# Row halves of the PE array in turn for RWKV preparation, and four quadrants for the token-pair products of the scan

## The chip, the cores and the metric

The kernel runs on one NeuronCore of a Trainium2 chip. The metric is device time in microseconds (us) of one execution. The kernel before was timed three times: 3051.62, 3055.73 and 3055.89 us, median 3055.73 us. Its profiled execution took 3055.24 us, of which the span of the trace is 3053.4 us; the remaining 1.8 us lie around the span.

## The reference

One inference step of a two-layer decoder. Each layer has three token mixers in parallel (retention, differential attention, RWKV-7), which are merged by gates, and an MLP. 512 prompt tokens and 8 single-token sequences (T = 520 columns) share all weights. The change touches only the RWKV-7 mixer. Cut to what matters (L is the layer, 8 heads of 64 channels):

```python
zs = z_rwkv + (zprev - z_rwkv) * mu_shift
rc, kc, vc, wd, ad, gd = split(zs)                      # 512, 512, 512, 64, 64, 160 columns
w = -softplus(-(w0 + tanh(wd) @ w_decay_up)) - 0.5      # contraction over 64
decay = exp(-exp(w))
vgate = sigmoid(v0 + (vc @ w_v_down) @ w_v_up)          # 512 -> 32 -> 512
vc = vc + (v_first - vc) * vgate                        # second layer only
a = sigmoid(a0 + ad @ w_a_up)                           # contraction over 64
kk = normalised(kc * k_k);  kc = kc * (1 + (a - 1) * k_a)
for t in tokens:                                        # S is 64 x 64 per head
    S = S * decay_t + (S @ -kk_t) outer (kk_t * a_t) + v_t outer k_t
    y_t = S @ r_t
y = groupnorm(y) + sum(r * k * r_k) * v                 # sum(r*k*r_k) is the "bonus"
```

The prompt scan is computed in chunks of 64 tokens. Within a chunk it needs the products of every pair of tokens, for every head: (b, a), (b, r), (k, a), (k, r), each a 64x64 block, then the inverse of a triangular matrix, then the update of the state chunk by chunk.

## The kernel before, in words

The layer body is one loop iteration; it consists of blocks, and all five engines meet at the end of each. Channels lie on partitions and tokens on columns for all of the preparation; a 520-column row is handled as two halves of 260 (`TH`), half h in PSUM banks 4h to 4h+3. All matmuls here are float32, and each appears in the trace as two MATMUL records, each with its LDWEIGHTS record, all at line 381 (transposes at 384). A form such as `64*128 64x260` means 64 rows and 128 columns of weights, and a moving operand of 260 columns. Engines order themselves by semaphores; `dv(...)` and `ac(...)` make VectorE and ScalarE wait for their own last instruction.

**The preparation block** (from line 1652) runs in this order. PE turns the previous rows, then adds up the squares of k for each head into four 32-column groups of the output (`pair32`). After that `up_tile` (line 1709) makes nine tiles: for n = 1 to 4 tanh(wd) times `w_decay_up` on rows 0 to 63, for n = 5 to 8 ad times `w_a_up` on rows 64 to 127. They alternate between two banks (`pair(n)`), and ScalarE's `tile` (line 1761) reads each with a sigmoid (`L1768`) and frees the bank. When all eight are read, ScalarE forms a factor (`L1794`), VectorE multiplies k by it (`L1876`), scans the decays (`L1880`) and scales kk by its norm (`L1886`). PE then makes `vc @ w_v_down`, eight matmuls of 32 output columns that add up in rows 0 to 31 of one bank pair. ScalarE copies these 32 rows (`L1770`), and four `up_tile` calls with 32 rows of weights give the gate of v, each read by a sigmoid. VectorE blends v (`L1896`, `L1898`) and forms r*k*r_k (`L1900`). PE sums that over heads with 20 small matmuls into bank 5 (the bonus), then turns 40 blocks of `dvec`, the operands of the 8 single tokens. VectorE forms z2 (`L1909`), waits for the bonus, copies it (`L1912`, `L1913`), multiplies z1, k and r by decays (`L1915`, `L1916`, `L1919`), and splits the turned blocks (`L1923`). SyncE issues the loads of the block's weights in the order of the code, and PE waits for all of them with one count (`loaded`, six loads of 16).

**A block for the eight single tokens** follows, which the change leaves alone.

**The scan block** (from line 2049) handles four groups m of 128 tokens, two chunks cc of 64 each. `products(left, right, m, bank, g)` makes for one row half g (channels of the even or the odd heads) eight 64x64 blocks: the rows of the array are those of g, the columns are those of cc, and cc alternates. The two calls of a pair (g = 0, then g = 1) write to two neighbouring banks. For each m: the blocks of (b, a) and (b, r) come first, then (k, a), five levels of `head_products` with masks on VectorE between them, (k, r) inside level 1, then for each cc the right-hand side, the update, the output and the new state. The (b, a) or (b, r) products of m+1 stand inside that last part: g = 0 ahead of the wait for `rhs_copied` and g = 1 behind the matmuls for `u`. VectorE masks (`L2164`, `L2185`), adds (`L2199`, `L2201`), copies the right-hand side (`L2206`) and `u` (`L2208`) and updates the state (`L2215`).

Of the kernel before, what the change touches and what calls it, by code (L numbers as in the profile page):

```python
# [20 lines left out]
ACT = mybir.ActivationFunctionType  # L21
AX = mybir.AxisListType

P = 128
# [3 lines left out]
MT = SEQ // P  # L28
DEC = 8
T = SEQ + DEC  # L30
TH = T // 2
# [6 lines left out]
HC, DC = 8, 64  # L38
HP = HC // 2
# [165 lines left out]
def build(nc, a, consts, outs):  # L205
# [6 lines left out]
    V, S, G, PE = nc.vector, nc.scalar, nc.gpsimd, nc.tensor  # L212
    with ExitStack() as ctx:
# [166 lines left out]
        def mm(out, lhsT, rhs, start=True, stop=True):  # L380
            return PE.matmul(out, lhsT, rhs, start=start, stop=stop, skip_group_check=True)  # L381
# [133 lines left out]
        with nc.Fori(0, DEPTH) as l:  # L515
# [1050 lines left out]
            w_g1, w_g2 = ring[1][:, 512:1024], ring[1][0:32, 1024:1536]  # L1566
            w_vu = ring[1][0:32, 1536:2048]
            w_vd = at(ring[1], 2048, HP, 32)
# [81 lines left out]
            ds_ = at(ring[0], 0, DEC, HP, DC)  # L1650
            decay_rate = -math.exp(-0.5)
            with nc.Block() as block:
                @block.sync
                def _(sp):
                    sp.dma_start(w_up2[0:64, :], L("w_decay_up")).then_inc(loaded, 16)
                    sp.dma_start(w_up2[64:128, :], L("w_a_up")).then_inc(loaded, 16)
                    sp.dma_start(w_vu, a["w_v_up"][0]).then_inc(loaded, 16)
                    sp.dma_start(w_vd, a["w_v_down"][0].rearrange("(k p) n -> p k n", p=P)).then_inc(loaded, 16)
                    sp.wait_ge(prev_turned, 1)
                    sp.dma_start(y3.rearrange("p k t -> p (k t)"), v_spill).then_inc(v_first_loaded, 16)  # L1660
                    wg = L("w_g_up")
# [12 lines left out]
                    sr = L("state_rwkv").rearrange("b (q g) i j -> g i b q j", g=2)  # L1674
                    for g in range(2):
                        for b in range(DEC):
                            sp.dma_start(ds_[g * 64:(g + 1) * 64, b], sr[g, :, b]).then_inc(states_loaded, 16)
                    sp.wait_ge(loaded, c["loaded"].base + 96)
                    sp.wait_ge(stored, c["stored"].next(32))
# [4 lines left out]
                def _(pe):  # L1684
# [13 lines left out]
                    def pair(n):  # L1698
                        return (pb[n % 2][:, 0:TH], pb[4 + n % 2][:, 0:TH])
# [8 lines left out]

                    def up_tile(n, lhs, rows_, rhs, ct):
                        for half in range(2):  # L1710
                            t = mm(pair(n)[half], lhs[rows_, ct * P:(ct + 1) * P], rhs[rows_, half * TH:(half + 1) * TH])
                        t.then_inc(up_made, 1)

                    pe.wait_ge(loaded, c["loaded"].base + 96)
                    pe.wait_ge(rows_copied, 3)
                    for n in range(1, 9):
                        if n >= 2:
                            pe.wait_ge(up_read, n - 1)
                        up_tile(n, w_up2, slice(0, 64) if n < 5 else slice(64, 128), wdad, (n - 1) % 4)

# [12 lines left out]
                    for half in range(2):  # L1733
                        for k in range(HP):
                            t = mm(pair(1)[half][0:32], w_vd[:, k, :], v_[:, k, half * TH:(half + 1) * TH],
                                   start=(k == 0), stop=(k == HP - 1))
                    t.then_inc(up_made, 1)
                    pe.wait_ge(kk_scaled, 4)
                    for ct in range(HP):
                        pe.wait_ge(up_read, 10 + max(0, ct - 1))  # L1740
                        up_tile(ct, w_vu, slice(0, 32), vdn, ct)

                    pe.wait_ge(dve_for_pe, c["pe_from_dve"].next())
                    for m in range(5):
                        r = P if m < MT else DEC
                        for hp in range(HP):
                            t = mm(pb[5][0:r, m * 8 + hp * 2:m * 8 + hp * 2 + 2], y3[:, hp, m * P:m * P + r], C("pair"))
                    t.then_inc(pe_for_dve, 1)
                    pe.wait_ge(dve_for_pe, c["pe_from_dve"].next())
                    for n in range(5):  # L1750
                        for hp in range(HP):
                            for g in range(2):
                                gs, c0 = slice(g * 64, (g + 1) * 64), n % 2 * 256 + hp * DC
                                t = mm(pb[n // 2][32 * g:32 * (g + 1), c0:c0 + DC], dvec[gs, n, hp, :], ident[gs, gs])
                    t.then_inc(pe_for_act, 1)

                @block.scalar
                def _(s):
# [26 lines left out]
                    for n in range(1, 9):  # L1785
                        ct = (n - 1) % 4
                        tile(n, n % 2, (z0 if n < 5 else z1)[:, ct], ACT.Sigmoid, name=PR("w0" if n < 5 else "a0")[:, ct:ct + 1])
                        if n in (4, 8):
                            S.sem_inc(act_for_dve, 1)


# [5 lines left out]
                    
                    tile(9, 1, vdn, ACT.Copy, rows_=32)
                    s.wait_ge(dve_for_act, c["act_from_dve"].next())
# [23 lines left out]
                def _(v):  # L1823
# [86 lines left out]
                    V.sem_inc(dve_for_act, 1)  # L1910
                    v.wait_ge(pe_for_dve, c["dve_from_pe"].next())
                    V.tensor_copy(bonus[:, 0:MT], at(pb[5], 0, MT, HC))  # L1912
                    dv(V.tensor_copy(bonus[0:DEC, MT], pb[5][0:DEC, MT * 8:MT * 8 + 8]))  # L1913
                    v.wait_ge(act_for_dve, c["dve_from_act"].next())
# [5 lines left out]
                    for i in range(3):  # L1920
# [3 lines left out]
                                           tokv[0][:, nn].bitcast(F32), sub))  # L1924
            c["loaded"].skip(96)

# [122 lines left out]
            with nc.Block() as block:  # L2049

                @block.tensor
                def _(pe):
                    def products(left, right, m, bank, g):

                        gs = slice(g * 64, (g + 1) * 64)
                        for hp in range(HP):
                            for cc in range(2):
                                tok = slice(m * P + cc * CH, m * P + (cc + 1) * CH)
                                t = mm(at(pb[bank + g], 0, HP, CH)[lower[cc], hp], left[gs, hp, tok], right[gs, hp, tok])
                        return t  # L2060
# [7 lines left out]

                    products(z1, z2, 0, 4, 0)
                    products(z1, z2, 0, 4, 1).then_inc(ba_made, 1)  # L2070
                    products(z1, r_, 0, 6, 0)
                    products(z1, r_, 0, 6, 1).then_inc(br_made, 1)
                    for m in range(MT):
# [8 lines left out]
                        pe.wait_ge(ba_masked, m + 1)  # L2082
                        products(k_, z2, m, 4, 0)
                        products(k_, z2, m, 4, 1).then_inc(ka_made, 1)
                        for lv in range(1, 6):
# [6 lines left out]
                            if lv == 1:  # L2092

                                pe.wait_ge(br_masked, m + 1)
                                products(k_, r_, m, 6, 0)
                                products(k_, r_, m, 6, 1).then_inc(kr_made, 1)
                            for g in range(2):
# [10 lines left out]
                        for cc in range(2):  # L2108
# [15 lines left out]
                            if m + 1 < MT:  # L2124
                                products(z1, (z2, r_)[cc], m + 1, 4 + 2 * cc, 0)
                            pe.wait_ge(rhs_copied, n + 1)
                            for h, hp, g, hs, gs in heads:
                                t = mm(pb[1][r, hs], xt[r, g, hp], rhs1[r, hs])
                            t.then_inc(u_made, 1)
                            if m + 1 < MT:  # L2130
                                products(z1, (z2, r_)[cc], m + 1, 4 + 2 * cc, 1).then_inc((ba_made, br_made)[cc], 1)
                            if n:
# [587 lines left out]
```

## Time and profile before

| | |
|---|---|
| median of 3 runs | 3055.73 us (3051.62 to 3055.89) |
| profiled execution | 3055.24 us, span 3053.4 us, mean granted clock of TensorE 0.895 |
| PE busy | 2675.8 us, 88% of the span |
| VectorE busy | 1466.5 us, 48% |
| ScalarE busy | 828.7 us, 27% |
| preparation block, first layer | about 708 to 786.5 us |
| single-token block, first layer | about 786.5 to 831.6 us |
| scan block, first layer | from 831.6 us to about 987 us |

Times in a trace are counted from the start of the span. The granted clock is a share of full speed: 1.00 is 2.4 GHz and 0.50 is 1.2 GHz. In a timeline, `xN` merges N neighbouring instructions, whose duration is from the start of the first to the end of the last, and the bracket gives the idle time of the engine just before and what ended it. Matmuls are pipelined, so the busy share of PE does not tell how full its array is.

### The profile page before, as it was taken

The numbers are of one execution on the slowest core, as the hardware profiler recorded it, in microseconds if no ns is written. First come the engines' busy times: TensorE is split into PE (matmuls) and PEld (weight loads), VectorE is DVE, ScalarE is ACT, GpSimd is POOL, SyncE is SP. The second block draws the span as 40 slices with busy tenths as digits, with TensorE's granted clock in tenths as the row PEclk, the third lists the DMA queues.
The fourth block names the chain that finished last, engine by engine and source line by source line (L and its number), as shares of the span: only waits on it lengthen the run. The fifth ranks groups of instructions, "written<-read, shape, count | busy, mean of one in ns | idle before, by whom it ended". The sixth has DMA issues, their size and how long they took to land. (4 is left out here: it accounts for less than half of the span.)

```text
span 3053.4 us, 52943 instructions
## 1 busy us (share of the span) xinstructions
PE 2675.8 (88%) x22778; PEld 2336.9 (77%) x22778; DVE 1466.5 (48%) x2077; ACT 828.7 (27%) x1232; POOL 164.0 (5%) x102
## 2 busy tenths in 40 slices
PE   5988888997698898999979879798958979799998
PEld 3777665895587698999956767577936859799998
DVE  4253256434755765334351632734366566633343
ACT  1311224223310332333232112332241114232331
POOL 0021010300000000000000210112000000000000
PEclk8987899996599799999989879889956979899999
DMA  7222245711000442222341331655010015322223
GB/s 290 69 66 78 88 166 191 224 45 53 15 3 4 144 161 76 91 84 84 138 150 35 87 117 46 232 183 178 21 48 15 3 45 181 111 84 83 84 83 139
DMA packets 216308, 305.14 MB, mean 100 GB/s; under 512 B 28021, under 2 KB 97191, under 8 KB 214786
## 3 DMA queue, kind: packets, MB, share of 16 engines
q1 hardware_dynamic: 216066, 301.67, 29.6%
q8 instruction: 182, 2.98, 0.4%
q14 instruction: 60, 0.49, 0.0%
HBM read 266.49 MB, written 35.14 MB: 99 GB/s over the span
## 5 line engine op out<-in xcount | busy, mean ns | idle before, releaser
L381 PE MATMUL pb<-h_high,f_high 128*128 128x260 f32 x1984 | 400.9, 283 | 4.9 <-DVEq L2641 4.9
L381 PE MATMUL pb<-h_low,f_high 128*128 128x260 f32 x1984 | 398.1, 282 | 0.0
L381 PE MATMUL pb<-h_high,f_low 128*128 128x260 f32 x1920 | 387.2, 283 | 0.0
L556 DVE TENSOR_TENSOR w_low<-ring,w_high 128x2048 fp32r<-128x2048 f32 x66 | 151.3, 2292 | 379.2 <-ACT w_high L548 377.8
L381 PEld LDWEIGHTS pb<-h_high,f_high 128*128 128x128 f32 x1984 | 305.7, 188 | 5.3 <-issue 5.3
L381 PEld LDWEIGHTS pb<-h_low,f_high 128*128 128x128 f32 x1984 | 307.1, 189 | 0.0
L556 DVE TENSOR_TENSOR f_low<-ring,f_high 128x2048 fp32r<-128x2048 f32 x60 | 137.6, 2293 | 337.1 <-ACT h_high L550 212.8
L381 PEld LDWEIGHTS pb<-h_high,f_low 128*128 128x128 f32 x1920 | 294.0, 188 | 0.0
L763 POOL TENSOR_TENSOR g_low<-yT,g_high 128x512 fp32r<-128x512 f32 x96 | 161.8, 1691 | 1942.6 <-ACT g_high L759 1942.6
L548 ACT ACTIVATE f_high<-ring 128x2048 fp32r<-128x2048 f32 x62 | 118.8, 1916 | 350.9 <-PE pb L381 326.5
L381 PE MATMUL pb<-arena 64*64 64x64 f32 (+4 forms) x2320 | 190.8, 302 | 23.7 <-DVE arena L987 9.4
L548 ACT ACTIVATE w_high<-ring 128x2048 fp32r<-128x2048 f32 x66 | 126.1, 1916 | 308.1 <-PE pb L381 185.7
L381 PE MATMUL pb<-h_high,g_high 128*128 128x260 f32 x768 | 165.9, 299 | 41.6 <-POOL g_low L763 21.9
L381 PE MATMUL pb<-w_high,h_high 128*128 128x512 f32 x448 | 183.2, 409 | 21.7 <-DVEq L560 11.6
L381 PE MATMUL pb<-h_high,w_high 128*128 128x260 f32 x800 | 167.4, 292 | 31.6 <-DVE h_low L2535 17.1
L381 PEld LDWEIGHTS pb<-arena 64*64 64x64 f32 (+4 forms) x2320 | 143.6, 170 | 59.3 <-issue 39.2
L381 PE MATMUL pb<-w_high,h_low 128*128 128x512 f32 x448 | 179.9, 401 | 0.0
L381 PE MATMUL pb<-w_low,h_high 128*128 128x512 f32 x448 | 179.8, 401 | 0.0
L381 PEld LDWEIGHTS pb<-h_high,g_high 128*128 128x128 f32 x768 | 124.1, 198 | 60.8 <-POOL g_low L763 38.9
L381 PE MATMUL pb<-h_high,w_low 128*128 128x260 f32 x800 | 165.1, 288 | 0.0
L381 PE MATMUL pb<-h_low,w_high 128*128 128x260 f32 x800 | 164.9, 288 | 0.0
L381 PE MATMUL pb<-h_low,g_high 128*128 128x260 f32 x768 | 160.0, 291 | 0.0
(368 smaller groups left out, 4631.6 us busy)
## 6 DMA issues: line engine op xcount, KB each, us to landing
ring<-in_w_ff_dram SPq DMA_DIRECT2D x32, 2048.0 KB, 8.0
ring<-in_w_in_dram SPq DMA_DIRECT2D x20, 2048.0 KB, 8.9
ring<-in_w_ada_dram SPq DMA_DIRECT2D x18, 2048.0 KB, 8.4
yT<-in_w_in_dram SPq DMA_DIRECT2D x96, 256.0 KB, 3.5
arena<-in_w_ada_dram SPq DMA_DIRECT2D x9, 2048.0 KB
gate_spill_dram<-yT SPq DMA_DIRECT2D x48, 260.0 KB, 4.1
arena<-gate_spill_dram SPq DMA_DIRECT2D x12, 1040.0 KB, 5.3
arena<-in_cache_k_diff_dram SPq DMA_DIRECT2D x32, 256.0 KB, 3.0
```

The lines of the kernel that those rows point to most:

```text
L381: return PE.matmul(out, lhsT, rhs, start=start, stop=stop, skip_group_check=True)
L548: t = S.activation(ws[n % 2][0], ring[slot][:, u * 2048:(u + 1) * 2048], ACT.Copy)
L556: t = V.tensor_tensor(ws[n % 2][1], ring[slot][:, u * 2048:(u + 1) * 2048], ws[n % 2][0].bitcast(F32), sub)
L763: G.tensor_tensor(g_split[j % 2][1], g_raw[j % 2], g_split[j % 2][0].bitcast(F32), sub).then_inc(gate_ready, 1)
```

## The change

In the preparation, the tiles of decay (rows 0 to 63) and of a (rows 64 to 127) are made in pairs over four bank pairs. The down-projection of v no longer adds up its four parts in PSUM: part k goes to output rows 32k to 32k+31, all 128 rows are copied, and `w_v_up` is loaded four times, one copy for each part, so that the up-projection adds them up with 128 rows of weights. The turning of `dvec` goes ahead of the bonus on PE, and VectorE copies the bonus last. In the scan, one call of `products` makes both row halves, in the order (g, cc) = (0,0), (1,1), (0,1), (1,0), and the products for m+1 all stand ahead of the wait for `rhs_copied`.

```diff
@@ preparation: operands, SyncE
-            w_vu = ring[1][0:32, 1536:2048]
+            w_vu = ring[1][:, 1536:2048]
...
+            def up_bank(ct, x):
+
+                return (2 + x) if ct % 2 == 0 else (1 - x)
...
-                    sp.dma_start(w_vu, a["w_v_up"][0]).then_inc(loaded, 16)
+                    for k in range(HP):
+                        sp.dma_start(w_vu[32 * k:32 * (k + 1), :], a["w_v_up"][0]).then_inc(loaded, 16)
@@ preparation: PE
-                    pe.wait_ge(loaded, c["loaded"].base + 96)
+                    pe.wait_ge(loaded, c["loaded"].base + 144)
                     pe.wait_ge(rows_copied, 3)
-                    for n in range(1, 9):
-                        if n >= 2:
-                            pe.wait_ge(up_read, n - 1)
-                        up_tile(n, w_up2, slice(0, 64) if n < 5 else slice(64, 128), wdad, (n - 1) % 4)
+                    for ct in range(HP):
+                        if ct:
+                            pe.wait_ge(up_read, (1, 2, 4)[ct - 1])
+                        for half in range(2):
+                            for x in range(2):
+                                rows_ = slice(64 * x, 64 * (x + 1))
+                                if half == 0 and ct >= 2 and x:
+                                    pe.wait_ge(up_read, 2 * ct - 1)
+                                t = mm(pb[4 * half + up_bank(ct, x)][:, 0:TH], w_up2[rows_, ct * P:(ct + 1) * P],
+                                       wdad[rows_, half * TH:(half + 1) * TH])
+                                if half:
+                                    t.then_inc(up_made, 1)
...
-                            t = mm(pair(1)[half][0:32], w_vd[:, k, :], v_[:, k, half * TH:(half + 1) * TH],
-                                   start=(k == 0), stop=(k == HP - 1))
+                            t = mm(pair(1)[half][32 * k:32 * (k + 1)], w_vd[:, k, :], v_[:, k, half * TH:(half + 1) * TH])
...
-                        up_tile(ct, w_vu, slice(0, 32), vdn, ct)
-
-                    pe.wait_ge(dve_for_pe, c["pe_from_dve"].next())
-                    for m in range(5):
...
-                    t.then_inc(pe_for_dve, 1)
-                    pe.wait_ge(dve_for_pe, c["pe_from_dve"].next())
+                        up_tile(ct, w_vu, vdn, ct)
+
+                    pe.wait_ge(dve_for_pe, c["pe_from_dve"].next(2))
                     for n in range(5):
...
                                 t = mm(pb[n // 2][32 * g:32 * (g + 1), c0:c0 + DC], dvec[gs, n, hp, :], ident[gs, gs])
                     t.then_inc(pe_for_act, 1)
+                    for m in range(5):
+                        r = P if m < MT else DEC
+                        for hp in range(HP):
+                            t = mm(pb[5][0:r, m * 8 + hp * 2:m * 8 + hp * 2 + 2], y3[:, hp, m * P:m * P + r], C("pair"))
+                    t.then_inc(pe_for_dve, 1)
@@ preparation: ScalarE
-                        ct = (n - 1) % 4
-                        tile(n, n % 2, (z0 if n < 5 else z1)[:, ct], ACT.Sigmoid, name=PR("w0" if n < 5 else "a0")[:, ct:ct + 1])
+                        ct, x = (n - 1) // 2, (n - 1) % 2
+                        tile(n, up_bank(ct, x), (z0, z1)[x][:, ct], ACT.Sigmoid, name=PR(("w0", "a0")[x])[:, ct:ct + 1])
...
-                    tile(9, 1, vdn, ACT.Copy, rows_=32)
+                    tile(9, 1, vdn, ACT.Copy)
@@ preparation: VectorE
                     dv(V.scalar_tensor_tensor(z2, kk, -1.0, z0, mult, mult))
                     V.sem_inc(dve_for_act, 1)
-                    v.wait_ge(pe_for_dve, c["dve_from_pe"].next())
-                    V.tensor_copy(bonus[:, 0:MT], at(pb[5], 0, MT, HC))
-                    dv(V.tensor_copy(bonus[0:DEC, MT], pb[5][0:DEC, MT * 8:MT * 8 + 8]))
...
                                            tokv[0][:, nn].bitcast(F32), sub))
+                    v.wait_ge(pe_for_dve, c["dve_from_pe"].next())
+                    V.tensor_copy(bonus[:, 0:MT], at(pb[5], 0, MT, HC))
+                    dv(V.tensor_copy(bonus[0:DEC, MT], pb[5][0:DEC, MT * 8:MT * 8 + 8]))
@@ scan: PE
-                    def products(left, right, m, bank, g):
-                        gs = slice(g * 64, (g + 1) * 64)
+                    def products(left, right, m, bank):
                         for hp in range(HP):
-                            for cc in range(2):
+                            for g, cc in ((0, 0), (1, 1), (0, 1), (1, 0)):
+                                gs = slice(g * 64, (g + 1) * 64)
                                 tok = slice(m * P + cc * CH, m * P + (cc + 1) * CH)
                                 t = mm(at(pb[bank + g], 0, HP, CH)[lower[cc], hp], left[gs, hp, tok], right[gs, hp, tok])
...
                             if m + 1 < MT:
-                                products(z1, (z2, r_)[cc], m + 1, 4 + 2 * cc, 0)
+                                products(z1, (z2, r_)[cc], m + 1, 4 + 2 * cc).then_inc((ba_made, br_made)[cc], 1)
                             pe.wait_ge(rhs_copied, n + 1)
                             for h, hp, g, hs, gs in heads:
                                 t = mm(pb[1][r, hs], xt[r, g, hp], rhs1[r, hs])
                             t.then_inc(u_made, 1)
-                            if m + 1 < MT:
-                                products(z1, (z2, r_)[cc], m + 1, 4 + 2 * cc, 1).then_inc((ba_made, br_made)[cc], 1)
```

The other three pairs of calls of `products` become one call each in the same way.

## Rows read from the trace of the kernel before

**Rows 1.** The page's first line on engines: busy us, share of span, instructions.
```profile
PE 2675.8 (88%) x22778; PEld 2336.9 (77%) x22778; DVE 1466.5 (48%) x2077; ACT 828.7 (27%) x1232; POOL 164.0 (5%) x102
```

**Rows 2.** Windows: stretch, length, busy us (instructions) by engine, PEclk, DMA.
```profile
723.20:735.60 12.40, 12.25 (x30) 8.47 (x30) 4.90 (x2) 6.79 (x17) 0.00 (x0) 0.50 0.47 122
746.00:762.00 16.00, 12.56 (x40) 6.92 (x40) 8.66 (x13) 4.46 (x11) 0.00 (x0) 0.71 0.00 1
762.00:786.50 24.50, 11.14 (x120) 10.93 (x120) 18.97 (x20) 9.72 (x10) 0.00 (x0) 0.57 0.00 1
2224.90:2237.30 12.40, 12.24 (x30) 8.48 (x30) 4.86 (x2) 6.77 (x16) 0.00 (x0) 0.50 0.46 121
```

**Rows 3.** Timeline of the preparation, 718 to 762: start, us, engine, line, tiles.
```profile
718.30 1.96 PE L381 MATMUL pb<-arena,cst 128*32 128x260 f32 x16 [5.32 <-ACTq L1779]
720.19 3.83 PE L381 MATMUL pb<-rstd,ring 64*128 64x260 f32 x8
723.23 1.81 ACT L1768 ACTIVATE arena<-pb,par 128x260 f32<-128x260 f32 x4
724.17 10.38 PE L381 MATMUL pb<-rstd,ring 64*128 64x260 f32 x24 [0.15 <-ACTq L1772]
734.59 0.85 ACT L1768 ACTIVATE arena<-pb,par 128x260 f32<-128x260 f32 x2 [0.89 <-PE pb L381]
738.77 2.33 DVE L1876 TENSOR_TENSOR arena<-xT,arena 128x2080 f32<-128x2080 f32 x1 [10.53 <-ACTq L1796]
749.88 4.96 PE L381 MATMUL pb<-arena,ring 128*32 128x260 f32 x16
755.71 1.99 PE L381 MATMUL pb<-arena,ring 32*128 32x260 f32 x8 [0.87 <-ACTq L1772]
761.71 2.38 DVE L1896 SCALAR_TENSOR_TENSOR yT<-arena,cst,yT 128x2080 f32<-128x2080 f32 x1 [5.18 <-ACTq L1802]
```

**Rows 4.** Timeline of the preparation's end, 769 to 786.
```profile
769.38 7.26 PE L381 MATMUL pb<-cst,yT 128*128 128x2 f32 x40 [8.90 <-DVEq L1902]
772.45 1.94 ACT L1812 ACTIVATE arena<-xT 128x2080 f32<-128x2080 f32 x1 [6.07 <-DVEq L1910]
776.57 3.94 PE L381 MATMUL pb<-cst,arena 64*32 64x64 f32 x80
776.68 0.19 DVE L1912 COPY small<-pb 128x32 f32<-128x32 f32 x1 [4.33 <-PE pb L381]
777.13 2.33 DVE L1915 TENSOR_TENSOR arena<-arena 128x2080 f32<-128x2080 f32 x1 [0.20 <-DVE small L1913]
784.18 1.85 DVE L1923 TENSOR_TENSOR tok_low<-pb,tok_high 64x512 fp32r<-64x512 f32 x3
```

**Rows 5.** Timeline row of SyncE; below it GB/s of 706 to 735 in 40 slices.
```profile
709.42 0.58 SPq L1657 DMA_DIRECT2D ring<-in_w_v_up_dram  x1
...
GB/s 0 0 0 0 20 209 204 187 117 311 436 402 344 232 3 0 0 0 0 0 40 142 344 413 367 295 129 108 94 90 90 86 84 78 83 71 79 79 84 90
```

**Rows 6.** The scan: two windows, then timeline rows.
```profile
831.60:834.00 2.40, 2.38 (x64) 2.40 (x64) 2.38 (x2) 2.02 (x8) 0.00 (x0) 0.50 0.03 7
875.40:878.80 3.40, 3.40 (x92) 3.40 (x90) 1.60 (x4) 0.29 (x1) 0.00 (x0) 0.50 0.00 0
...
831.62 2.32 DVE L2157 TENSOR_TENSOR h_low<-yT,h_high 128x2080 fp32r<-128x2080 f32 x1 [5.54 <-PEq L1935]
867.74 0.63 PE L381 MATMUL pb<-arena 64*64 64x64 f32 x13
868.21 1.09 PE L381 MATMUL pb<-arena,ring 64*64 64x64 f32 x16
871.05 0.42 DVE L2215 TENSOR_TENSOR ring<-ring,pb 128x256 f32<-128x256 f32 x1 [2.41 <-PE pb L381]
949.77 1.03 PE L381 MATMUL pb<-arena 64*64 64x64 f32 x31
953.30 1.28 PE L381 MATMUL pb<-arena 64*64 64x64 f32 x25
```

More of the change, by code:

```diff
@@ L1677, in _ @@
                             sp.dma_start(ds_[g * 64:(g + 1) * 64, b], sr[g, :, b]).then_inc(states_loaded, 16)
-                    sp.wait_ge(loaded, c["loaded"].base + 96)
+                    sp.wait_ge(loaded, c["loaded"].base + 144)
                     sp.wait_ge(stored, c["stored"].next(32))
@@ L1707, in _, with up_tile @@
                     t.then_inc(up_made, 1)
-                    def up_tile(n, lhs, rows_, rhs, ct):
+                    def up_tile(n, lhs, rhs, ct):
                         for half in range(2):
-                            t = mm(pair(n)[half], lhs[rows_, ct * P:(ct + 1) * P], rhs[rows_, half * TH:(half + 1) * TH])
+                            t = mm(pair(n)[half], lhs[:, ct * P:(ct + 1) * P], rhs[:, half * TH:(half + 1) * TH])
                         t.then_inc(up_made, 1)
-                    pe.wait_ge(loaded, c["loaded"].base + 96)
+                    pe.wait_ge(loaded, c["loaded"].base + 144)
                     pe.wait_ge(rows_copied, 3)
-                    for n in range(1, 9):
-                        if n >= 2:
-                            pe.wait_ge(up_read, n - 1)
-                        up_tile(n, w_up2, slice(0, 64) if n < 5 else slice(64, 128), wdad, (n - 1) % 4)
+                    for ct in range(HP):
[10 more added lines that the diff above has]
+                                    t.then_inc(up_made, 1)
                     pe.wait_ge(kk_factor, 1)
@@ L1740, in _ @@
                         pe.wait_ge(up_read, 10 + max(0, ct - 1))
-                        up_tile(ct, w_vu, slice(0, 32), vdn, ct)
-                    pe.wait_ge(dve_for_pe, c["pe_from_dve"].next())
-                    for m in range(5):
-                        r = P if m < MT else DEC
-                        for hp in range(HP):
-                            t = mm(pb[5][0:r, m * 8 + hp * 2:m * 8 + hp * 2 + 2], y3[:, hp, m * P:m * P + r], C("pair"))
-                    t.then_inc(pe_for_dve, 1)
-                    pe.wait_ge(dve_for_pe, c["pe_from_dve"].next())
+                        up_tile(ct, w_vu, vdn, ct)
+                    pe.wait_ge(dve_for_pe, c["pe_from_dve"].next(2))
                     for n in range(5):
@@ L1785, in _ @@
                     for n in range(1, 9):
-                        ct = (n - 1) % 4
-                        tile(n, n % 2, (z0 if n < 5 else z1)[:, ct], ACT.Sigmoid, name=PR("w0" if n < 5 else "a0")[:, ct:ct + 1])
-                        if n in (4, 8):
-                            S.sem_inc(act_for_dve, 1)
+                        ct, x = (n - 1) // 2, (n - 1) % 2
+                        tile(n, up_bank(ct, x), (z0, z1)[x][:, ct], ACT.Sigmoid, name=PR(("w0", "a0")[x])[:, ct:ct + 1])
+                    S.sem_inc(act_for_dve, 2)
                     s.wait_ge(dve_for_act, c["act_from_dve"].next())
@@ L1924, in _ @@
                                            tokv[0][:, nn].bitcast(F32), sub))
-            c["loaded"].skip(96)
+                    v.wait_ge(pe_for_dve, c["dve_from_pe"].next())
+                    V.tensor_copy(bonus[:, 0:MT], at(pb[5], 0, MT, HC))
+                    dv(V.tensor_copy(bonus[0:DEC, MT], pb[5][0:DEC, MT * 8:MT * 8 + 8]))
+            c["loaded"].skip(144)
             ytok = at(x_raw, 0, 5, 512)
@@ L2067, in head_products @@
                         return t
[L2069 to L2072, printed above, removed]
+                    products(z1, z2, 0, 4).then_inc(ba_made, 1)
+                    products(z1, r_, 0, 6).then_inc(br_made, 1)
                     for m in range(MT):
@@ L2082, in _ @@
                         pe.wait_ge(ba_masked, m + 1)
-                        products(k_, z2, m, 4, 0)
-                        products(k_, z2, m, 4, 1).then_inc(ka_made, 1)
+                        products(k_, z2, m, 4).then_inc(ka_made, 1)
                         for lv in range(1, 6):
@@ L2094, in _ @@
                                 pe.wait_ge(br_masked, m + 1)
-                                products(k_, r_, m, 6, 0)
-                                products(k_, r_, m, 6, 1).then_inc(kr_made, 1)
+                                products(k_, r_, m, 6).then_inc(kr_made, 1)
                             for g in range(2):
```

## The prediction, made before the changed kernel was built

> **What bounds the kernel now.** I read the page's totals first: PE is busy for 88% of the span and VectorE for 48% [rows 1]. The average says little here, so I went to the windows of the blocks that the change touches. In 12.4 us of the first layer's preparation PE is never idle, yet its clock is 0.50, and the second layer repeats it to 0.01 us [rows 2]; every sum below is made for one layer and doubled. The timeline then shows what each wait ends on [rows 3, 4]. The preparation is one chain over three engines with little slack: VectorE sits idle for 10.53 us before L1876 until ScalarE's factor comes, ScalarE waits 0.89 us for PE before each sigmoid tile, later VectorE waits 5.18 us for the gate of v and 4.33 us for the bonus. In the scan the waits are shorter and mostly on PE: 2.41 us before the state update [rows 6]. Every block ends where all engines meet, so what a chain gains inside its block reaches the end of the kernel.
>
> **Sigmoid tiles.** Eight tiles of two matmuls, four records each: 8 records take 3.83 us and 24 take 10.38 us, 0.4325 us a record (260 columns in two passes at 1.2 GHz), so a tile costs PE 4 x 0.4325 = 1.73 us against 0.85 us on ScalarE [rows 3]. All run on one row half at a time. With the halves in turn PE makes two tiles in 1.73 us, if they overlap. No row shows two 64-row forms of this size side by side; the nearest ones do show that tiles of the array run together: 16 records on four different 32-column groups take 1.96 us, four at a time [rows 3]. Bounds: no overlap, 0 gained; full overlap, and ScalarE sets the pace. I take the second. ScalarE's 4 reads took 1.81 us when nothing held them [rows 3]; with a little between tiles I say 0.95 us a tile. From 723.23 that gives 723.23 + 8 x 0.95 = 730.8, where the last read now ends at 734.59 + 0.85 = 735.4. Gain 4.6 us. The first pair starts at 720.2 as now, and is ready before the table load ends at 723.2; the later waits for freed banks fall 1 to 2 us ahead of their tile.
>
> **Three more loads.** SyncE issues `w_v_up` four times instead of once, at 0.58 us each: the loads behind it, that of v_first included, are issued 1.7 us later. Traffic of these loads ends by 706 + 14 x 0.725 = 716.2 [rows 5], so by about 717.9 afterwards; PE wants them at 720.19 [rows 3]. Cost 0, with 2.3 us of cover. Without it the cost would be at most 1.7 us a layer.
>
> **Down- and up-projection of v.** The down-projection has 16 records on one column group, 4.96 us [rows 3]. On four groups it has the form of the 1.96 us row. Gain 3.0 us. It now starts at 749.88, thus at 745.3 after the gain above, and ends at 747.2. The copy by ScalarE is of 128 rows instead of 32, same columns, same time; I keep the 0.87 us between the two steps [rows 3], so the up-projection starts at 748.1. It has 16 records as before, with 128 rows instead of 32. Their time hangs on the clock. The window around them averages 0.71 now [rows 2]. From 755.71 to VectorE's start at 761.71 it takes 6.0 us, less than 16 records would take at 1.2 GHz (16 x 0.4325 = 6.9 us), so PE runs mostly at the high clock. If that stays, VectorE can start at 754.1, a gain of 7.6 us in all. If all 16 records run at 1.2 GHz they take 6.9 us, plus the last read of 0.85 us and some 0.6 us of waits: 756.4, a gain of 5.3 us. VectorE itself is free at 761.71 - 5.18 - 4.6 = 751.9, so it does not bound this. I take 7.0: the array is fuller than before, which speaks for the high clock, but the pause around the copy speaks against it.
>
> **The bonus goes last.** Now 40 records of the bonus take PE 7.26 us, VectorE waits 4.33 us for them, and the turning of dvec (3.94 us) follows [rows 4]. Afterwards VectorE waits at L1915 for z0 alone, which ScalarE has ready at 772.45 + 1.94 = 774.4. Say 774.55 instead of 777.13: 2.6 us. The rest of its queue keeps its length. The dvec results are ready earlier, and ScalarE's copies of them fit beside VectorE's three multiplications of 2.33 us. The bonus on PE ends 3.94 + 7.26 = 11.2 us after 769.38, thus at 780.6, before VectorE is through with its split at 774.55 + 1.85 + 784.18 - 777.13 = 783.5. The clock of this stretch is 0.57 [rows 2], so I leave PE's durations as they are. The two copies of the bonus cost about 0.35 us at the end. Net gain 2.2 us; were the bonus late, less, down to 0.
>
> Preparation: 7.0 + 2.2 = 9.2 us a layer.
>
> **Products in the scan.** A 64-column record occupies its quadrant for 0.4325 x 64/260 = 0.107 us at 1.2 GHz; at 2.4 GHz sixteen records on one quadrant start over 1.09 - 0.22 = 0.87 us, 0.058 us each [rows 6] (0.22 is the length of the last). A pair of calls has 32 records, 8 on each quadrant: 0.86 us at the low clock and 0.47 us at the high one, if all four quadrants run together. But today's order is not serial either: 64 records at the low clock took 2.38 us, 1.2 us a pair, and 31 at the high clock took 1.03 - 0.31 = 0.72 us [rows 6]. PE looks far enough ahead to start g = 1 beside g = 0. So a pair gains 0.25 to 0.35 us, not half.
> The first two pairs of a layer gain nothing: VectorE is in its 2.32 us split until 833.94 [rows 6]. In the levels, (k, a) and (k, r) lie on PE's chain, partly at 0.50 [rows 6]; the (k, r) records at 953.30 spread over almost 1 us. Between 0.2 and 0.9 us for each m; I take 0.4, so 1.6 us a layer.
> In the part by cc, the pair for m+1 now stands whole ahead of `u`. A row half has 8 + 8 records in turn on each quadrant before `u`, 16 x 0.058 = 0.93 us, which is what the copy of the right-hand side covers already; `u` is then late by 0 to 0.1 us. Behind `u`, for cc = 1, the 13 records at 867.74 hold back the next group on the same quadrant until 868.21: 0.47 us go [rows 6], on the way to the state update that VectorE waits 2.41 us for. For cc = 0 the two use different quadrants and only 0.1 us goes. Three m: 3 x 0.57 = 1.7 us. If the quadrants do not overlap further, `u` comes 0.3 us later for each cc and this part gains 0.
> Scan: 3.3 us a layer, bounds 0 and 5.
>
> The sum: 2 x (9.2 + 3.3) = 25.0 us. 3055.24 - 25 = 3030.2 us on the profiled execution, which lies 0.5 us under the median of 3055.73; I say 3030.5.
>
> **A rule weighed.** The rows of 0.72 us for 31 records mean a start every 23 ns. The Trainium skill (TensorE: Matmul & The Clock Gate, "Wait — 56ns, not 53.3ns?") says that starts of matmuls never come closer than about 25 ns, however small they are. By that rule 32 records can't take less than 0.8 us, and the scan gains nothing from its four quadrants. The four-wide row of 1.96 us does not decide it, having only 16 records; in it the starts come four together, which speaks against a strict floor.
>
> **The rivals.**
> *Issue bound.* The 23 ns a record at 949.77 may be what PE can issue and not what its quadrants allow. For it: two quadrants at 0.058 us would give 29 ns, so 23 is near to it already. Against it: at the low clock 64 records take 37 ns each, so the rate follows the clock. Then the scan gains 0: 3055.24 - 18.4 = 3036.8. Chance 0.15.
> *Row halves don't overlap.* Then the tiles stay at 1.73 us each; the rest gains 4.6 us a layer less: 3039.4. For it: PE never shows the case. Against: the scan's two row halves do overlap, as just seen. Chance 0.08.
> *The clock stays low in the up-projection.* 5.3 instead of 7.0: 3.4 us less, 3033.6. Chance 0.12, the measurement hardly tells it from the forecast.
> *Slower: the scan falls to the low clock.* After the pause at a group boundary PE runs at 1.2 GHz for a stretch of 3.4 us [rows 6]. Packing the same work denser leaves longer pauses. A stretch of 3.4 us at half speed costs up to 1.7 us of PE's chain; with 15 more of them over the eight groups m the gain is gone, and with 20 the time is 3055.24 - 25 + 34 = 3064.2. Against it: PE's pauses here grow by only 0.3 us each. Chance 0.03.
>
> **How the numbers follow.** Forecast 0.62, rivals 0.15, 0.08, 0.12, 0.03. The forecast's own spread (3026 to 3034) comes from the clock in the up-projection (-1.2 to +3.4 us), the levels (0.2 to 0.9 us for each m) and stretches of clock that shift by a window in the untouched blocks behind. The range reaches from 3024 to 3040, to hold the first three rivals too. A measurement tells a change of 0.2%, 6 us, from none: under 3049.6 is faster. Even both non-overlaps together (3055.24 - 9.2 = 3046) stay under that; only the slower rival and what lies between it and them do not: faster 0.94, same 0.03, slower 0.03.
>
> **What would show it.** The sigmoid tiles on ScalarE follow each other without 0.89 us gaps, and L1876 starts 4.6 us earlier relative to the block's start. The down-projection is one row of about 2 us. VectorE does not wait before L1915 beyond ScalarE, and L1912 is last in the block. Blocks: preparation 9 us shorter, single tokens unchanged, scan 3.3 us shorter. A pair of products shows 32 records in 0.5 us at the high clock. The prediction is wrong if the tiles keep a pitch of 1.73 us, if pairs of products keep their 0.7 us, or if most windows of the scan show a granted clock of 0.50.

## The result, and the profile after

The kernel after the change took 3023.81 us (median of 4 runs, 3015.62 to 3027.65) beside 3055.81 us for the kernel before, which has a fourth run here (3051.62 to 3057.19). The ratio is 0.9894, 95% interval 0.987 to 0.9918. Another set of runs on another occasion gave 3026.42 beside 3049.53 us, ratio 0.9918 (0.99 to 0.9937). Single runs of one kernel differ by up to 14 us, so the parts are read from the blocks' lengths in the traces, which repeat to 0.1 us as long as the clock falls the same way.

The profiled execution took 3026.71 us, span 3024.9 us: 28.5 us less than the one before, where the forecast had 25.0. The lengths below are differences between starts of instructions on VectorE. "Low" is short for time at the granted clock of 0.50, 1.2 GHz. The preparation runs from the copy of the last rows to the first clear of the single-token block. The scan runs from the split of h_low to the last copy. A group ends at the second state update.

| us, first / second layer | before | after | difference | forecast |
|---|---|---|---|---|
| preparation | 72.90 / 72.90 | 64.24 / 64.21 | -8.66 / -8.69 | -9.2 |
| single tokens | 44.93 / 45.02 | 45.22 / 45.22 | +0.29 / +0.20 | 0 |
| scan | 155.71 / 155.80 | 150.24 / 150.22 | -5.47 / -5.58 | -3.3 |
| start and all else | | | -0.6 | 0 |

The preparation after, PE and ScalarE (timeline):

```profile
722.59 2.87 PE L381 MATMUL pb<-rstd,ring 64*128 64x260 f32 x16
...
725.62 7.62 ACT L1780 ACTIVATE arena<-pb,par 128x260 f32<-128x260 f32 x16
...
747.68 1.96 PE L381 MATMUL pb<-arena,ring 128*32 128x260 f32 x16
750.55 5.97 PE L381 MATMUL pb<-arena,ring 128*128 128x260 f32 x16 [0.91 <-ACTq L1784]
766.11 4.48 PE L381 MATMUL pb<-cst,arena 64*32 64x64 f32 x80 [9.59 <-DVEq L1918]
770.52 7.26 PE L381 MATMUL pb<-cst,yT 128*128 128x2 f32 x40
```

The eight tiles are one unbroken row of 16 reads of 7.62 us on ScalarE, where [rows 3] had a wait of 0.89 us before a tile. PE makes four of the tiles, 16 records, in 2.87 us. A part of that is at the high clock, but the overlap does not rest on it: while the clock is still 0.50, the records of the two row halves start 7 ns apart, and the next two follow 0.43 us later. The row halves do overlap. The down-projection is the 1.96 us form that the forecast took from [rows 3], and the bonus now stands behind the turned blocks. VectorE after:

```profile
716.19 0.45 DVE L1858 COPY ring<-pb 9x288 f32<-9x288 f32 x1
736.57 2.32 DVE L1886 TENSOR_TENSOR arena<-xT,arena 128x2080 f32<-128x2080 f32 x1 [5.93 <-ACTq L1806]
757.84 2.38 DVE L1906 SCALAR_TENSOR_TENSOR yT<-arena,cst,yT 128x2080 f32<-128x2080 f32 x1 [3.50 <-ACTq L1812]
770.58 2.33 DVE L1922 TENSOR_TENSOR arena<-arena 128x2080 f32<-128x2080 f32 x1 [2.10 <-ACTq L1823]
779.52 0.19 DVE L1933 COPY small<-pb 128x32 f32<-128x32 f32 x1
780.43 0.48 DVE L2021 MEMSET arena<- 128x512 f32 x1 [0.67 <-PEq L1657]
```

This block starts 2.4 us later than before (716.19 against 713.79), from work ahead of the change. Counted from there the wait of 10.53 us at the factor is 5.93 us, L1906 comes 6.3 us earlier, and L1922 waits for ScalarE, no longer for the bonus, whose copy ends the block without a wait.

The scan after: VectorE's start, the second state update of each of the four groups and the last copy, and then windows over the four groups (columns as in [rows 2]):

```profile
825.65 2.33 DVE L2161 TENSOR_TENSOR h_low<-yT,h_high 128x2080 fp32r<-128x2080 f32 x1 [5.84 <-PEq L1945]
863.42 0.42 DVE L2219 TENSOR_TENSOR ring<-ring,pb 128x256 f32<-128x256 f32 x1 [1.95 <-PE pb L381]
899.84 0.42 DVE L2219 TENSOR_TENSOR ring<-ring,pb 128x256 f32<-128x256 f32 x1 [1.95 <-PE pb L381]
937.12 0.42 DVE L2219 TENSOR_TENSOR ring<-ring,pb 128x256 f32<-128x256 f32 x1 [1.95 <-PE pb L381]
973.29 0.42 DVE L2219 TENSOR_TENSOR ring<-ring,pb 128x256 f32<-128x256 f32 x1 [1.95 <-PE pb L381]
975.89 0.42 DVE L2227 COPY arena<-pb 128x256 f32<-128x256 f32 x1 [0.84 <-PE pb L381]
```

```profile
825.70:863.40 37.70, 34.48 (x885) 32.19 (x886) 22.93 (x52) 3.31 (x11) 0.00 (x0) 0.90 0.01 3
863.40:899.80 36.40, 33.53 (x836) 31.15 (x834) 21.30 (x52) 3.97 (x12) 0.00 (x0) 0.95 0.01 3
899.80:937.10 37.30, 34.54 (x836) 32.30 (x835) 21.30 (x52) 3.97 (x12) 0.00 (x0) 0.91 0.01 3
937.10:973.30 36.20, 32.73 (x772) 30.04 (x771) 20.66 (x51) 5.77 (x20) 0.00 (x0) 0.95 0.01 3
```

Two windows of the kernel before, over its third and fourth group:

```profile
908.40:945.70 37.30, 34.44 (x835) 31.98 (x834) 21.32 (x52) 3.97 (x12) 0.00 (x0) 0.95 0.01 3
945.70:984.70 39.00, 34.94 (x772) 32.11 (x771) 20.66 (x50) 5.77 (x20) 0.00 (x0) 0.91 0.01 3
```

A mean clock of 0.95 is 3.4 us at 1.2 GHz in the window, 0.91 is 6.8 us. The fourth group lost 2.8 us (39.0 to 36.2) and half its low clock. The third has the same 37.3 us as before, but with twice the low clock. So the lengths of single groups mix code and clock, and the experiments have to part them. The update wait of 2.41 us [rows 6] is 1.95 us. Products of a pair at the high clock, inside the fourth group:

```profile
943.96 0.63 PE L381 MATMUL pb<-arena 64*64 64x64 f32 x30
```

Start to start that is 0.63 - 0.22 = 0.41 us for 30 records, 14 ns each, against 0.72 us for 31 [rows 6]. The first two records of the pair stand 0.10 us ahead of this row, in a row of their own. Counted from single starts, all 32 take 0.52 us at the high clock, 17 ns each, where the kernel before takes 0.82 us for the pair at 949.67; at the low clock it is 0.95 us (pair at 831.58) against 1.45 us (at 837.53). So a pair gains 0.3 us at the high clock and 0.5 us at the low one.

### The profile page after: what moved, and what is told of

Its sections match the earlier page's. It is cut to its first block and busy times, and to the rows that moved or that the text cites. A ratio compares the mean times of both kernels' runs of the same rounds, so it can differ in the third digit from the quotient of the medians.

```text
span 3024.9 us, 52947 instructions
## 1 busy us (share of the span) xinstructions
PE 2646.0 (87%) x22778; PEld 2315.8 (77%) x22778; DVE 1465.6 (48%) x2077; ACT 828.0 (27%) x1232; POOL 165.2 (5%) x102
## 5 line engine op out<-in xcount | busy, mean ns | idle before, releaser
L381 PE MATMUL pb<-h_high,g_high 128*128 128x260 f32 x768 | 167.5, 301 | 43.1 <-POOL g_low L763 23.4
L381 PE MATMUL pb<-arena 64*64 64x64 f32 (+4 forms) x2320 | 173.9, 299 | 24.1 <-DVE arena L987 9.4
L381 PEld LDWEIGHTS pb<-arena 64*64 64x64 f32 (+4 forms) x2320 | 129.7, 168 | 61.2 <-issue 41.2
```

## The experiments

Two theories on what the scan gained beyond its forecast. **A:** the length of the scan hangs on where its groups begin against the steps of TensorE's clock; the kernel before stood badly there, and the shorter preparation moved it. **B:** the denser products themselves gain it.

**Only the preparation.** The scan's code is that of before.

```diff
-                        up_tile(n, w_up2, slice(0, 64) if n < 5 else slice(64, 128), wdad, (n - 1) % 4)
...
+                                t = mm(pb[4 * half + up_bank(ct, x)][:, 0:TH], w_up2[rows_, ct * P:(ct + 1) * P],
+                                       wdad[rows_, half * TH:(half + 1) * TH])
...
+                            t = mm(pair(1)[half][32 * k:32 * (k + 1)], w_vd[:, k, :], v_[:, k, half * TH:(half + 1) * TH])
...
+                    pe.wait_ge(dve_for_pe, c["pe_from_dve"].next(2))
```

> Only the preparation is changed; the scan is that of before. Both theories: the preparation block (from VectorE's copy of the last rows to the first instruction of the single-token block) falls from 72.9 to 64.2 us a layer, some 17 us in all, and the single tokens stay at 45 us. Theory A (the scan's extra gain over the 3.3 us a layer of the forecast is a stretch of low clock in the last group of tokens, which hangs on when the group begins against the steps of the clock): with the scan beginning some 6 to 9 us earlier, its last group may show 3.4 instead of 6.8 us of low clock and the scan 154 instead of 155.7 us. Theory B (the extra gain comes from the products themselves): the scan stays at 155.7 us with 6.8 us of low clock in the last group.

Measured: 3030.79 us, ratio 0.9931 (0.991 to 0.9953). Preparation 64.24 us, scan 152.94 us. Its fourth group, with unchanged code:

```profile
942.70:979.80 37.10, 33.80 (x772) 30.96 (x771) 20.67 (x51) 5.76 (x20) 0.00 (x0) 0.95 0.01 3
```

39.0 us have become 37.0 with the scan's code as it was, and the clock of the window is 0.95 instead of 0.91. B is out for this part: in this run the scan is 2.8 us a layer shorter without any change to it. A had expected 1.7 us; the rest is mostly the first group, which has 6.8 us of low clock instead of 9.6 and takes 38.7 instead of 39.4 us.

**Only the scan.**

```diff
-                    def products(left, right, m, bank, g):
+                    def products(left, right, m, bank):
...
+                            for g, cc in ((0, 0), (1, 1), (0, 1), (1, 0)):
...
+                                products(z1, (z2, r_)[cc], m + 1, 4 + 2 * cc).then_inc((ba_made, br_made)[cc], 1)
                             pe.wait_ge(rhs_copied, n + 1)
```

> Only the scan is changed; the preparation is that of before, 72.9 us a layer. Theory A (the extra gain is a matter of when the last group begins against the clock's steps): the scan starts where it did before, the last group can keep its 6.8 us of low clock, and the scan takes about 152 us a layer, 3.5 us less than before, total about 3048. Theory B (the products themselves): the scan takes 150.2 us as in the full change, 5.5 us less a layer, total about 3045.

Measured: 3039.82 us, ratio 0.9967 (0.9951 to 0.9983), scan 148.67 and 149.06 us, better than either theory said. With the same code as in the full change it is 1.2 to 1.6 us shorter, again by the clock; its second group has none at the low level:

```profile
869.90:904.80 34.90, 32.03 (x835) 29.65 (x834) 21.11 (x52) 3.96 (x12) 0.00 (x0) 1.00 0.02 4
```

That supports A, but its guess of which way the clock would fall from the old starting moment was wrong: the product code changes when the later groups begin, too. The first group has the low clock of before (9.7 us) and is 0.9 us shorter, so the second begins 0.9 us sooner.

**Order alone.** In the full change, `products` goes back to one row half after the other.

```diff
-                        for hp in range(HP):
-                            for g, cc in ((0, 0), (1, 1), (0, 1), (1, 0)):
+                        for g, hp in ((g, hp) for g in range(2) for hp in range(HP)):
+                            for cc in range(2):
```

> The full change, but one call of products goes through the row halves one after the other again (g = 0 for all heads, then g = 1, cc alternating within), in the new place ahead of the wait. If the order over four quadrants is what gains (theory A and B alike), the scan gets slower than 150.2 us by 1.5 to 3 us a layer and a pair of products takes 0.7 us again at the high clock; the copies of the right-hand side no longer cover the pair, so u is later by about 0.3 us for each chunk. If PE is bound by issue (the rival of the prediction), nothing changes and the scan stays at 150.2 us.

Measured: scan 153.92 and 154.00 us. Groups of equal low clock (3.4 us) take 37.0 us here:

```profile
859.50:896.50 37.00, 34.13 (x835) 31.75 (x834) 21.32 (x52) 3.97 (x12) 0.00 (x0) 0.95 0.01 3
933.50:972.50 39.00, 35.03 (x773) 32.20 (x772) 20.68 (x51) 5.77 (x20) 0.00 (x0) 0.91 0.01 3
```

"Place" is where the products for m+1 stand (all ahead of the wait for `rhs_copied`), "order" the turn of the four quadrants. A middle group takes 37.34 us with the code of before, 37.02 with the new place, 36.42 with place and order. So the place gains 0.3 us and the order 0.6 us a group, taken in this sequence; the order at the old place was not run. The 0.3 is rough: over all traces, middle groups of the old code at 3.4 us low take 37.14 to 37.37 us. A pair at the high clock takes 0.75 us again, as expected, and PE was not bound by issue. The last group has 6.8 us of low clock again and takes as long as before, 38.94 us.

**The full change again.**

> The full change once more, for a second trace and a firmer ratio: both theories expect preparation 64.2 us and a median between 3016 and 3028 us. Theory A allows the scan's length to differ by 1.7 us from 150.2 in this trace where the low stretches fall differently; theory B expects 150.2 us again.

Measured: 3026.42 us, preparation 64.22 us, scan 150.20 and 150.22 us with the same low stretches. Neither block moved, which tells A and B apart no further. Why the clock falls the same way each time is not shown. That the code fixes the distance from preparation to scan is not enough, as the full change with a delayed scan shows below: there the distance is the same in both layers, and the low stretches are not.

**The three parts of the preparation**, one at a time on the kernel before.

```diff
@@ tiles alone
+                            for x in range(2):
+                                rows_ = slice(64 * x, 64 * (x + 1))
@@ v alone
+                            t = mm(pair(1)[half][32 * k:32 * (k + 1)], w_vd[:, k, :], v_[:, k, half * TH:(half + 1) * TH])
...
+                        up_tile(ct, w_vu, slice(0, 128), vdn, ct)
@@ bonus alone
+                    pe.wait_ge(dve_for_pe, c["pe_from_dve"].next(2))
```

> Only the sigmoid tiles go over the row halves in turn. Forecast: the preparation block takes 72.9 - 4.6 = 68.3 us a layer, ScalarE's sixteen reads follow each other. Rival (row halves do not overlap): 72.9.

> Only the down- and up-projection of v are changed, with the three more loads. Forecast for this part: 3.0 us from the down-projection, less up to 1.3 us if the up-projection runs at the low clock, which makes 71.2 to 69.9 us a layer. Rival (the clock takes all of it back): 72.9.

> Only the bonus goes behind the turned blocks, on PE and on VectorE. Forecast: 2.2 to 2.6 us less a layer, preparation 70.5 us. Rival (VectorE meets the late bonus at the end): 72.9.

Measured, preparation: tiles 68.38, v 70.92, bonus 70.52 us, so 4.5, 2.0 and 2.4 us less. Together 8.9 us, beside 8.7 in the full change. The rival of each forecast, 72.9 us, is out. Each run is also the scan of before at another moment: it took 152.3, 153.1 and 154.9 us.

**The kernel before, its scan delayed.**

```diff
-                    dv(V.memset(stc, 0.0))
+                    for _ in range(6):
+                        dv(V.memset(stc, 0.0))
```

> The kernel before, with five more clears of the small state tile on VectorE ahead of the scan's first mask, which delay the whole scan by about 1.7 us. Theory A (the scan's length hangs on when its groups begin against the clock's steps): some group changes its low stretches, above all the last one from 6.8 to 3.4 us, and the scan less its delay is 1 to 3 us off 155.7. Theory B (the products themselves): groups take 37.34, 37.34 and 38.99 us as before, and only the first is longer by the delay.

The six clears took 2.23 us instead of 0.27, a delay of 1.96 us:

```profile
833.89 2.33 DVE L2157 TENSOR_TENSOR h_low<-yT,h_high 128x2080 fp32r<-128x2080 f32 x1 [5.71 <-PEq L1935]
836.22 2.23 DVE L2159 MEMSET ring<- 128x256 f32 x6
```

The scan took 155.30 and 155.18 us with the delay in it, thus 153.3 without, against 155.7. The first group grew by only 1.2 us for the 1.96 us of delay (39.44 to 40.66), and the last one gave back 1.6 us, at 3.4 instead of 6.8 us low:

```profile
949.20:986.60 37.40, 33.71 (x772) 30.88 (x770) 20.67 (x51) 5.77 (x20) 0.00 (x0) 0.95 0.01 3
```

Theory A is shown here by itself, in a kernel without any of the change, and in both layers. The preparation of the first layer, whose code is that of before, took 75.7 us in this execution with 68.9 us of low clock, and 72.9 us in the second: it has such lengths too.

**The same delay in the full change.**

> The full change with the same delay of about 1.6 us on VectorE ahead of the scan's first mask. Theory A: the low stretches of the groups fall otherwise than 7.9, 3.4, 6.8, 3.4 us and the scan less its delay is off 150.2 by up to 2 us, in either direction. Theory B: groups 2 to 4 take 36.42, 37.29 and 36.16 us as before.

Measured: 153.86 us in the first layer and 151.01 us in the second, thus 151.9 and 149.1 without the delay. Here the groups' low stretches are 11.3, 0, 3.4, 9.8 us and 11.3, 0, 3.4, 0 us. One code can lie on either side, although preparation and single tokens took the same time in both layers (64.24 and 64.23, 45.23 us).

**The products behind u**, quadrant order kept.

```diff
-                            if m + 1 < MT:
-                                products(z1, (z2, r_)[cc], m + 1, 4 + 2 * cc).then_inc((ba_made, br_made)[cc], 1)
                             pe.wait_ge(rhs_copied, n + 1)
...
                             t.then_inc(u_made, 1)
+                            if m + 1 < MT:
+                                products(z1, (z2, r_)[cc], m + 1, 4 + 2 * cc).then_inc((ba_made, br_made)[cc], 1)
```

> The full change, but the products for the next group stand whole behind the matmuls for u, not ahead of the wait for the right-hand side. Forecast of the prediction for the place: up to 0.57 us a group, of which the run with serial order showed 0.3. Here u can start when the copy is done, and the next matmuls wait for the pair instead: groups 1 to 3 at the same low stretches take 0.3 to 0.9 us longer than 36.42 us, the last group is unchanged at 36.16.

Measured: scan 154.09 us, second and third group 37.20 and 37.26 us at 3.4 us low, 0.8 us more than ahead of the wait. As expected; only the last group, 38.44 us at 6.8 us low, was moved by the clock once more.

**Filler in PE's pauses**, in the full change.

```diff
                     for m in range(MT):
+                        for _ in range(4 if m else 3):
+                            mm(pb[2][:, 0:TH], ident, k_[:, 0, 0:TH])
```

> The full change, with filler matmuls (128x128 weights, 260 columns, into a bank that is overwritten later; their result is not used) in PE's pause at the start of each group of the scan: three for the first group, four for each later one, about as long as the pause. Theory A (the low clock at the start of a group costs 0.9 to 2.0 us a stretch, and PE's pause brings it on): the stretches of 3.4 us in groups 2 to 4 go, groups take about 34.9, 34.9 and 34.6 us instead of 36.4, 37.3 and 36.2, and the scan about 145 us instead of 150.2, some 10 us less in all: about 3015. Theory B (the clock plays no part in the scan's length): PE is only fuller, the scan stays at 150.2 us or gets longer by what the filler overruns.

Measured: 3011.67 us (2999.63 to 3013.39), ratio 0.9873 (0.9856 to 0.9889), scan 145.26 and 145.32 us. The filler is eight records in front of the transposes, and three groups stay at 2.4 GHz from end to end:

```profile
860.28 2.02 PE L381 MATMUL pb<-arena,cst 128*128 128x260 f32 x8
862.27 1.42 PE L381 MATMUL pb<-cst,arena 64*64 64x64 f32 x30
```

```profile
859.50:894.40 34.90, 33.95 (x843) 31.08 (x842) 21.14 (x52) 3.97 (x12) 0.00 (x0) 1.00 0.01 4
894.40:929.50 35.10, 34.15 (x845) 31.29 (x843) 21.15 (x53) 3.97 (x12) 0.00 (x0) 1.00 0.01 4
929.50:965.60 36.10, 33.56 (x778) 30.29 (x777) 20.66 (x50) 5.77 (x20) 0.00 (x0) 1.00 0.01 3
```

The forecast of the scan was 145 us, the trace has 145.3 in both layers. A group without a low stretch takes 34.9 us with filler and 34.9 us without it (the second group of the run with only the scan changed), so the gain is the clock's. All four runs lie under all eight of the full change (3015.62 to 3029.04), though they were taken on another occasion. The profiled run, 2999.63 us, is the fastest of the four: 17.8 us of its distance to the kernel before lie outside the preparations, single tokens and scans, and are no gain of the filler. The fourth group is at 36.16 us with or without a low stretch of 3.4 us: in both PE waits for ScalarE there, which has the bonus of two blocks to work off (here in the full change):

```profile
938.59 3.93 ACT L2239 ACTIVATE ring<-arena,small 128x64 f32<-128x64 f32 x16
```

## Why the prediction was right or wrong

The direction and the mechanisms that it named were right, and one that it did not count in the scan, the shift of the low clock, was missing. The sum of 25.0 us was 3.5 us short of the profiled pair, and 3023.81 lies 0.2 us under the range's lower end of 3024. The scan's term accounts for the 3.5 us and more. That the median also left the range is not all its doing: the profiled execution (3026.71) and the second median (3026.42) lie inside. The forecast's last addition is slightly off: 3030.2 plus 0.5 is 3030.7. By its own steps:

- **Sigmoid tiles**, -4.6: shown, -4.5. ScalarE sets the pace, at 7.62 us for eight tiles. The change also puts ScalarE's signal for the first four tiles behind the eighth, which the diff above leaves out; VectorE waited for both before L1876 as it was, so this costs nothing.
- **Three more loads**, 0: shown. PE starts on the tiles right behind the squares as before.
- **Down- and up-projection**: L1906 was forecast 7.0 us earlier, tiles included, and came 6.3 us earlier. The down-projection has its 1.96 us; the up-projection took 5.97 us, and PE was at the low clock for the first 4.5 us of it. Of the two bounds, 5.3 and 7.6, the value lies in the middle, and I had leaned to the wrong side. The part alone gained 2.0 us.
- **Bonus last**, -2.2: -2.4.
- **Preparation**, -9.2: -8.7.
- **Products in the scan**, -3.3 a layer: this is the step that failed, and the term that was mis-sized. It measured -5.5. At equal low clock the code gains 0.92 us in a middle group (37.34 to 36.42) where the forecast had 0.4 + 0.57 = 0.97, and 0.87 in the fourth (37.03 to 36.16) where it had 0.4. That part of the term, the pairs in the levels, was too small: it took 0.25 to 0.35 us a pair, from rows at the high clock, and at the low clock, where many of these pairs run, a pair gains 0.5 us. With about 1.0 us in the first group (38.77 at 8.0 us low in the run of v alone, 37.76 at 7.9 us after) the code makes about 3.7 us; fourth groups of the old code at 3.4 us low vary from 36.90 to 37.40 us, so this is good to some 0.5 us. The other 1.8 us a layer, 3.6 us in all, are clock: 39.0 to 37.0 us in the fourth group and some in the first, less about 0.9 us given back in the third. The forecast counted shifts of the clock only for the untouched blocks, as spread. In the scan it looked for them on the slow side alone, as longer pauses.
- **Place against order.** Of a middle group's gain the forecast gave the place 0.57 and the order 0.4; measured are 0.3 and 0.6. The sum was right by two errors, which is luck. Without further overlap of the quadrants it gave the place nothing; in the serial order it still gained its 0.3.
- **Issue bound**: out. The 32 records of a pair start 17 ns apart on average at the high clock, where 31 of the kernel before took 23 ns each. The Trainium skill (TensorE: Matmul & The Clock Gate, "Wait — 56ns, not 53.3ns?") has a floor of about 25 ns from start to start. The trace does not agree, and the measurement decides: four quadrants together run below it.
- **Row halves don't overlap**: out, by the 2.87 us row. **The slower rival**: low clock at the start of the groups is real and costs up to 2.0 us a stretch, but denser work did not add to it in this pair: 23.3 us low in the scan before, 21.6 after. Over all traces the old code has 17.1 to 23.4 us and the new one, without filler, 13.1 to 27.6, by the starting moment.

What stays open is why a median moved by 32.0 us on one occasion and by 23.1 on the other, where preparations, single tokens and scans add up to 27.9 in the trace of either occasion. Runs of one kernel spread over 12 to 14 us. The traces place such differences in blocks that the change does not touch: beside the kernel before, these are 8.4 us longer in the run of the preparation alone and 17.8 us shorter in that with filler. On the second occasion all three medians fall short of their blocks by about the same (23.1 for 27.9, 18.7 for 22.6, 9.7 for 13.7), which points to the median of the kernel before, 3049.53, rather than to the change. What moves those blocks was not looked into. Open is also what fixes the way the clock falls; the runs show that it depends on the moment at which the scan starts, not how.

## What to carry to other kernels

Where PE pauses for about 2 us at regular places in a chain, each pause may cost a stretch of half clock behind it, 0.9 to 2.0 us each here; then the length of the block depends on the moment at which it starts, by 3.4 us of 155 here, and any edit ahead of it seems to gain or lose in it. Compare pieces at equal low clock before a gain is put down to code, and try filler matmuls in the pauses. Small matmuls gain from the order of their quadrants even where PE overlaps them somewhat already, and they belong under a wait that another engine sets.

## What was not expected of the hardware

- The scan's code of before took 152.3 to 155.8 us in six traces (the delay taken out), with nothing changed in it but the moment at which it starts. In each of these traces its two layers agree to about 0.1 us. The new code agrees so in the full change and in its repetition, but not with the delay (153.86 and 151.01 us) or with the old preparation (148.67 and 149.06 us).
- 64-row matmuls on one row half kept PE without a pause for 12.4 us at 1.2 GHz [rows 2]. With both halves in turn the clock rose to 2.4 GHz after the first 1.7 us of tiles. PE then paused for part of the time, and the clock fell again behind that pause (rows below). This was no chance of one trace: in both layers of all eight traces with the tiles in turn the clock rose 1.5 to 1.9 us after the first tile, and in both layers of all five with the old tiles it stayed at 1.2 GHz for all 14.4 us of them. Which property of the work decides it was not tested.

```profile
722.60:724.20 1.60, 1.60 (x12) 1.16 (x8) 0.68 (x2) 1.53 (x3) 0.00 (x0) 0.50 0.28 41
724.40:727.60 3.20, 1.82 (x14) 0.95 (x12) 3.17 (x2) 2.94 (x6) 0.00 (x0) 1.00 0.95 342
727.80:731.00 3.20, 3.20 (x14) 2.19 (x12) 2.69 (x2) 2.83 (x8) 0.00 (x0) 0.50 0.44 97
```
